# Expert scores by matrix product instead of gathered rows, in a two-block transformer kernel

## The reference

```python
    q = (x @ w_peer_q).reshape(T, PEER_HEADS, PEER_DQ)
    s1, s2 = scores of the two halves of q with keys_1, keys_2      # 128 keys each
    v1, i1 = lax.top_k(s1, 16);  v2, i2 = lax.top_k(s2, 16)
    cand = v1[..., :, None] + v2[..., None, :]
    sc, ci = lax.top_k(cand, 16)
    eidx = e1 * 128 + e2                                            # 128 experts per token
    gates = softmax(sc)
    act = gelu(einsum('td,tkd->tk', xt, peer_u[it]))                # rows of 1024 float32
    y = einsum('tk,tkd->td', gt * act, peer_v[it])
```

## Time and profile before

| | us |
|---|---|
| median of 3 runs | 3166.22 (3160.13 to 3168.16) |
| the profiled execution | 3159.39 |
| its span | 3158.1 |
| TensorE, VectorE, GpSimd, ScalarE busy | 2272.4, 1802.2, 1432.2, 426.0 |
| mean granted TensorE clock | 0.81 |
| moved by DMA | 829.57 MB, of these 539.99 MB by GpSimd's queue |

### The profile page before, as it was taken

One profiled execution on the slowest core, in us unless ns is written; L12 is line 12 of the kernel. 1 busy time (PEld: TensorE's weight loads), 2 busy tenths in 40 slices (PEclk: granted clock), 3 DMA queues, 4 the chain that ended last, 5 costly groups with the idle time before them and its releaser, 6 DMA issues. The chain is left out here.

```text
span 3158.1 us, 24727 instructions
## 1 busy us (share of the span) xinstructions
PE 2272.4 (72%) x8222; PEld 1376.0 (44%) x8222; DVE 1802.2 (57%) x3876; ACT 426.0 (13%) x1209; POOL 1432.2 (45%) x1137
## 2 busy tenths in 40 slices
PE   5997980056673784767674478979957687969989
PEld 3535850023432662322344235758425443437544
DVE  1512119978779677566477897674666854224300
ACT  1212000011200100000000232012000321013310
POOL 0000002377667787778767764676655433100000
PEclk9796995577695796999885557989977688987999
DMA  3310522599889999978889877999998779942376
GB/s 129 121 67 27 173 96 101 157 350 370 282 337 329 333 401 352 321 237 266 293 306 398 288 249 230 394 386 393 363 360 330 259 246 379 340 153 83 126 259 220
DMA packets 291759, 829.57 MB, mean 263 GB/s; under 512 B 23568, under 2 KB 30016, under 8 KB 290864
## 3 DMA queue, kind: packets, MB, share of 16 engines
q0 software_dynamic: 148464, 539.99, 47.7%
q1 hardware_dynamic: 139872, 283.19, 24.7%
q10 hardware_dynamic: 3296, 4.80, 0.4%
HBM read 825.81 MB, written 2.10 MB: 262 GB/s over the span
## 5 line engine op out<-in xcount | busy, mean ns | idle before, releaser
L315 POOL DMA_INDIRECT picks_rows<-peer_u_dram,expert x512 | 723.5, 1413 | 830.2 <-DVE expert L1465 516.2
L315 POOL DMA_INDIRECT picks_rows<-peer_v_dram,expert x512 | 618.1, 1207 | 477.4 <-DVE h L380 354.6
L374 DVE CUSTOM_DVE_ANT_0 picks_rows<-picks_rows,xn 128x1024 f32<-128x1024 f32 x512 | 613.7, 1223 | 169.0 <-DMA picks_rows<-peer_u_dram,expert 144.4
L380 DVE SCALAR_TENSOR_TENSOR h<-picks_rows,picks_weight,h 128x1024 f32<-128x1024 f32 x416 | 535.0, 1286 | 189.4 <-DMA picks_rows<-peer_v_dram,expert 116.3
L465 PE MATMUL psum<-weight_ring,hnT 128*128 128x512 f32 (+4 forms) x576 | 236.9, 573 | 23.0 <-DMA weight_ring<-w_in_dram 10.9
L403 PE MATMUL psum<-picks_rows,picks_diag 128*128 128x512 f32 x384 | 187.3, 625 | 59.9 <-POOL picks_diag L333 59.5
L1753 PE MATMUL psum<-weight_ring,aT 128*128 128x512 f32 x512 | 220.8, 593 | 3.1 <-ACT aT L2060 1.4
L465 PEld LDWEIGHTS psum<-weight_ring,hnT 128*128 128x128 f32 (+1 forms) x576 | 106.2, 187 | 152.4 <-issue 137.5
L874 PE MATMUL psum<-identity_sb,na_probs 128*128 128x128 f32 (+2 forms) x384 | 93.7, 359 | 100.9 <-DVE na_probs L958 79.4
L656 PE MATMUL psum<-identity_sb,n_scaled 128*128 128x128 f32 (+1 forms) x104 | 24.1, 412 | 181.9 <-DVE n_scaled L640 181.9
L1753 PEld LDWEIGHTS psum<-weight_ring,aT 128*128 128x128 f32 x512 | 96.9, 190 | 125.3 <-issue 120.5
(11 more groups left out here) (353 smaller groups left out, 3170.8 us busy)
## 6 DMA issues: line engine op xcount, KB each, us to landing
weight_ring<-w_ff_dram SPq DMA_DIRECT2D x48, 2048.0 KB, 11.0
weight_ring<-w_in_dram SPq DMA_DIRECT2D x44, 2048.0 KB, 13.6
weight_ring<-w_proj_nsa_dram SPq DMA_DIRECT2D x6, 2048.0 KB, 8.1
weight_ring<-w_out_dram SPq DMA_DIRECT2D x6, 2048.0 KB, 14.8
weight_ring<-w_ret_out_dram SPq DMA_DIRECT2D x4, 2048.0 KB, 8.0
weight_ring<-w_mix_out_dram SPq DMA_DIRECT2D x4, 2048.0 KB, 18.9
weight_ring<-w_peer_q_dram SPq DMA_DIRECT2D x4, 2048.0 KB, 13.4
picks_rows<-peer_u_dram,expert POOLq DMA_INDIRECT x512, 7.8
```

The lines of the kernel that those rows point to most:

```text
L315: pool.indirect_dma_start(out=self.rows[:, n % GATHERS, :], out_offset=None, in_=table, in_offset=bass.IndirectOffsetOnAxis(ap=self.expert ...
L374: ins = nc.vector.tensor_tensor_reduce(out=row, in0=row, in1=self.x[t], scale=1.0, scalar=0.0, op0=ALU.mult, op1=ALU.add, accum_out=self.d ...
L380: ins = nc.vector.scalar_tensor_tensor(out=h, in0=row, scalar=self.weight[:, t % 2, k:k + 1], in1=h, op0=ALU.mult, op1=ALU.add)
```

## The change

**Scores.** `peer_select_stage` goes; `experts_stage` does both tiles of a wave. Beside the choice on VectorE, TensorE multiplies the normed tokens with all of `peer_u`, laid out on the host as 32 slabs of 1024 x 512. ScalarE copies each 128 x 512 piece out of PSUM into one of 4 buffers and stores it to a DRAM table, one per tile.

**Gathers.** The `u` gathers of rows and their VectorE steps go. After the stores of a wave have landed, GpSimd gathers the 128 picked scores of each of the two tiles, one float32 per token and DMA, and after these the `v` rows of both tiles. VectorE does all `v` steps; the diagonal products on TensorE and their instructions on GpSimd go. All 8 PSUM banks serve the stages.

**Shares.** The list of steps is 512 long (128 `v` steps per tile). They now belong to m1 to ex of the second wave of the first block (66, 24, 10, 24, 132 steps) and to m2 to nf of the first wave of the second block (36, 24, 10, 83, 96, 7).

```diff
-BANKS = 6
-V_BANKS = (6, 7)
+BANKS = 8
 SHARES = {
-    "sel1": 24, "n1_1": 13, "lat_1": 13, "nq_1": 9, "nkv_1": 9, "up_1": 12, "qk_1": 16, "tq_1": 6, "tk_1": 5, "ma2_1": 26,
...
+    "m1_1": 66, "mix_1": 24, "np_1": 10, "pq_1": 24, "ex_1": 132, "m2_0": 36, "out2_0": 24, "n32_0": 10, "ff12_0": 83,
+    "ff22_0": 96, "nf2_0": 7}
 GATHERS = 8
-DIAGS = 4
-DIAG_LAG = 5
+STAGES = 4
...
+        one += [(("pu", c), a["peer_u"][c], n) for c in range(SLABS)]
...
+    def issue(self, pool, tiles, stored):
+        for signal in stored:
+            pool.wait_ge(*signal)
+        for t in tiles:
+            self.gather_scores(pool, t, range(PICKS))
+        for t in tiles:
+            for k in range(PICKS):
+                self.gather_values(pool, t, k)
...
+    def gather_scores(self, pool, t, picks):
+        for k in picks:
+            if k == 0:
+                pool.wait_ge(self.expert_ready, t + 1)
             pool.indirect_dma_start(
+                out=self.dots[:, t, k:k + 1], out_offset=None, in_=self.scores[t],
+                in_offset=bass.IndirectOffsetOnAxis(ap=self.place[:, t, k:k + 1], axis=0),
+            ).then_inc(self.dots_landed[t], 16)
...
+        def tensor(pe):
+            g.begin(pe)
+            for c, name in enumerate(names):
+                if c == 0:
+                    keys(pe, 0)
+                if c == next_keys and n > 1:
+                    keys(pe, 1)
+                w = g.w.view(name)
+                g.w.arrived(pe, name)
+                for j in range(n):
+                    i = n * c + j
+                    if i >= 4:
+                        pe.wait_ge(*s_copied.after(i - 3))
+                    for k in range(KT):
+                        mm = nc.tensor.matmul(bank(i), xnT[:, k, P * j:P * j + P], w[:, k, :], start=(k == 0), stop=(k == KT - 1))
+                    mm.then_inc(g.w.products_done, 1)
...
+                    nc.scalar.copy(staged[:, i % STAGES, :], bank(i)).then_inc(s_copied.sem, 1)
+                    act.wait_ge(*s_copied.after(i + 1))
+                    rows = g.picks.scores[t].rearrange("(p e) o -> p (e o)", p=P)
+                    act.dma_start(rows[:, 512 * c:512 * c + 512], staged[:, i % STAGES, :]).then_inc(s_stored[i % STAGES].sem, 16)
```

More of the change, by code:

```diff
@@ L267, with __init__ @@
 class Picks:
-    def __init__(self, g, ctx, peer_u, peer_v, expert, gates):
+    def __init__(self, g, ctx, peer_v, scores, expert, place, gates):
         nc, self.g = g.nc, g
@@ L382, in use_to @@
-            ins.then_inc(self.taken["dve"], 1)
-    def add(self, pe, turn=None):
-        self.add_to(pe, self.last if turn is None else self.after(turn - 1))
-    def add_to(self, pe, end):
-        nc = self.g.nc
-        while self.added < end:
-            n = self.added
-            self.added += 1
-            if self.owner[n] != "pe":
-                continue
-            t, _, k = self.steps[n]
-            at = self.number[n] - 1
-            mine = [m for m in range(PICKS) if on_pe(t, m)]
-            if k == mine[0] and self.sums[t]:
-                pe.wait_ge(self.sum_added, self.sums[t])
-            pe.wait_ge(self.landed[n % GATHERS], 16 * (n // GATHERS + 1))
-            pe.wait_ge(self.diag_ready, at + 1)
-            for c, bank in enumerate(V_BANKS):
-                mm = nc.tensor.matmul(self.g.psum[:, bank, :], self.diag[:, at % DIAGS, :],
-                                      self.rows[:, n % GATHERS, 512 * c:512 * c + 512], start=(k == mine[0]), stop=(k == mine[-1]))
-            mm.then_inc(self.taken["pe"], 1)
@@ L407, in finish @@
-    def finish(self, act, dve, pe):
-        t, end = self.finished, 2 * PICKS * (self.finished + 1)
-        assert self.last >= end, (t, self.last)
+            if n:
+                dve.wait_ge(self.taken, n)
+            h = self.g.h[:, t, :]
+            self.g.nc.vector.scalar_tensor_tensor(out=h, in0=self.rows[:, n % GATHERS, :], scalar=self.weight[:, t % 2, k:k + 1],
+                                                  in1=h, op0=ALU.mult, op1=ALU.add).then_inc(self.taken, 1)
+    def finish(self, act, dve):
+        end = PICKS * (self.finished + 1)
+        assert self.last >= end, (self.finished, self.last)
@@ L898, in tensor @@
                 value(pe, s - 2)
-                g.picks.add(pe, 2 * min(s, steps))
-            g.picks.add(pe)
         def exponentials(act, s):
@@ L1477, in peer_select_stage @@
     for signal in (s_scores, s_over, s_exp):
-        signal.count += 1
-    g.ended["pe"], g.ended["act"], g.ended["dve"] = s_scores.after(0), s_exp.after(0), s_link.after(0)
-    g.picks.issue(nc.gpsimd, t)
+        signal.count += n
+    s_copied.count += n * SLABS
+    for i, signal in enumerate(s_stored):
+        signal.count += 16 * len(range(i, n * SLABS, STAGES))
+    g.ended["pe"], g.ended["act"], g.ended["dve"] = g.w.end(names[-1]), s_exp.after(0), s_link.after(0)
+    g.picks.issue(nc.gpsimd, tiles, [signal.after(0) for signal in s_stored])
 def picks_stage(g, tag):
@@ L2062, in second_wave @@
     rows = a["out"].rearrange("(t p) d -> p t d", p=P)
-    norm_stage(g, tag("nf"), [(g.h[:, t, :], P, None) for t in tiles], D, token_out=g.picks.x[first:last],
+    norm_stage(g, tag("nf"), [(g.h[:, t, :], P, None) for t in tiles], D, token_out=[rooms["xn"][:, t, :] for t in tiles],
                gain_rows=tables["g_final"], store=[rows[:, t, :] for t in tiles])
```

296 lines of the change are left out of this document (120 added, 176 removed), and 5 rows, old and new, of the table SHARES.

## The result

The changed kernel takes 3494.7 us (median of 4 runs, 3487.93 to 3495.72), the kernel before 3163.18 beside it: 1.1053 times the time before (95% interval 1.101 to 1.1096). The forecast was 3522, in a range of 3390 to 3660.

What follows compares the result with a forecast made beforehand. No engine was full throughout: TensorE set the pace at both ends, gathered rows and VectorE's picks between. Products (+888 us) and tables (+12), against stretches losing picks and partly waiting for gathers, gave 3522 us, range 3390 to 3660.

Steps and rivals of the forecast that it cites:

- three signs of being wrong: Small gathers above 1.5 us each; a scoring stage not near 444 us; MLP stages of tiles 0 and 1 keeping 224 us.
- step 5: Second block, tiles 0 and 1: merge at 2247 us, MLP stretched to about 335 us, tile 2's wave at 2768.
- Step 1: First scoring stage: products with all of peer_u take 444 us, 470 to 914, hiding DMA and choice; next wave at 935.
- Step 2: Second wave up to its merge, picks taken out: 263 us instead of 438, merge starting at 1198 us.
- Step 3: 256 small gathers ahead of value rows: 1.30 us each, 333 us; rows from 1253, then 85 MB in 230 us.
- Step 4: Second scoring stage: 444 us with 132 picks in it, its transfers of 404 us just hiding; end at 1932.
- Step 6: The last two waves: 369 us for tile 2's wave and 377 us for the last, ending at 3514.
- Rival A: Gathers never show: small ones done before the merges ask, value rows hide; 3249 us, chance 0.09.
- B: Small gathers are slow, up to 2.29 us each, 253 us more a wave: 4028 us, chance 0.10.
- C: Second scoring stage: slabs come late as stores, slabs and rows share engines; 510 instead of 444 us, 3588, chance 0.06.
- E: Scoring products cost one record each, not two; DMA holds the second scoring stage at 404 us; 3262 us, chance 0.02.
- D: TensorE the only bound once picks leave VectorE: 3075 us; faster only if its idle stays within 74 us; chance 0.03.

Runs made afterwards that it cites:

- The plain transfer: Changed kernel with one plain DMA of 128 neighbouring scores per tile instead of the 128 small gathers of picked ones: 3384.76 us, ratio 1.0714.

## Why the prediction was right

3494.7 us lies 27 under the forecast of 3522, and the steps that make up the sum came true, but for one. The prediction named three signs of being wrong, and the third came: the MLP stages kept their pace (step 5).

**Step 1, the products: right.** 444 us forecast a stage, 442 and 444 measured, 2048 records in 880 us, so 16 records in 6.88 us; the clock is 1.00, VectorE's choice and all copies lie beside it. The next wave began at 924, 11 us earlier than I had it: once the last stores had landed (917), exponential, gates and norm took 6.6 us where I had 15.

**Step 2, the stages without picks: right in kind, 18 us long.** Merge after 245 us from the first transposes (263 forecast). The longer keys in attention cost 9 us (54.9 against 46) where I added 17; the rest of the 18 I did not trace.

**Step 3, the small gathers: right.** 0.963 us on average and 0.30 behind, 1.26 against 1.30; the value rows at 1249.06 against 1253; VectorE's standstill from 1187 to 1253. Then I had 85 MB at 369 GB/s in 230 us. It was 208 us at 371 GB/s, so 77 MB; I take it that part of the slabs was there already. The plain transfer shows what this step costs the end, 110 us.

**Step 4: right.** 444 us with 132 picks in it, at 348 GB/s.

**Step 5: the sum right, the place wrong.** The merge came at 2176, not 2247: 20 us from the start of the stage, 12 because the gap behind the scoring stage was 23 us and not 35, and 40 because the stages without picks took 240 us where I took 280, near the lower bound of 237. This was one bad term, and it cost nothing: the first row is asked for at 2252 either way, 333 us of small gathers behind the scoring stage as forecast, and VectorE waited 64 us for it instead of the 8 that I had. The gathers of GpSimd were on the path. From there to tile 2's wave it took 486 us at 346 to 397 GB/s, forecast 497. But here the place was wrong. I had the MLP stretched to 335 us, and it took 226 at full pace, as in the kernel before (224): ScalarE drains its products, VectorE only does picks there, and slabs arrive in time. The deficit of picks showed as 116 us of idle TensorE behind the MLP. So the picture of a TensorE slowed by the picks inside the MLP is wrong, and the sum survived it for a reason and not by luck: the forecast of 497 us rests on the bytes, and these have to move before tile 2's wave wherever TensorE waits. Shares that move picks past that border get at the gap: 116 us became 13.

**Step 6: 367 and 382 us against 369 and 377.**

Rival A (gathers hide) failed on the queue, B (2.29 us each) on 0.963, C on the 444 us with rows and slabs together, E on 2048 records. D needs an idle TensorE of no more than 74 us; the kernel without picks, the best case of D, is at 3170 and no faster than before. Of the 27 us by which the span was forecast too long, 20 are there by the second scoring stage (4 at the rows, 16 behind them), 10 more by tile 2's wave, and the last two waves give 3 back.

One reading of mine does not carry over. I put the 1.99 us of a gather beside picks down to VectorE, with the Trainium skill (GPSIMD Engine Reference, section Specifications) behind it. GpSimd of the changed kernel, 44 us apart, beside VectorE's picks:

```profile
2628.64 1.73 POOL L311 DMA_INDIRECT picks_rows<-peer_v_dram,expert  x1 [0.30 <-issue]
...
2672.82 1.09 POOL L311 DMA_INDIRECT picks_rows<-peer_v_dram,expert  x1 [0.30 <-issue]
```

VectorE was busy 15.4 of 24 us beside the slow ones (2624 to 2648) and 22.2 of 24 beside the fast ones (2656 to 2680), so it is not what made them slow. What changed between them is that the last slab had landed. Until then slabs and rows shared the engines evenly (850 packets each from 2636 to 2648), and behind it only rows moved (1345 packets from 2656 to 2668). So most of a slow gather here goes with slabs in the transfers beside the rows, and the rule on the shared interfaces does not explain it. It may still hold for the 1.99 us of the earlier trace rows: there no slab moved (845 packets from 618 to 630, all of GpSimd's queue, at 257 GB/s), and no run tests that row.

## What to carry to other kernels

Before gathered rows are replaced by a dense product, compare it with what those rows cost the end (a run without them: 368 us) and not with their busy time or bytes: 682 us of a full engine can't win there, whatever is hidden. A gather's price on GpSimd is a turn in its queue, 1.25 us for 4 bytes a partition as for 4 KB while the transfers are not full, and small ones ahead of the rows delay everything behind them. Placing work in an in-order row pays only once its data can be there: the same shares cost 64 us with late rows (3494.7 to 3558.8), and with the order of the gathers changed they gained 68 (3446.2 to 3378.4).

## What the runs showed of the hardware that I had not expected

TensorE can start one record per 2.80 us, whatever its size, for 70 us and more at a time. It did so in the profiled execution of the kernel with half the products (the other one was 18 us shorter, so it must have too), at a granted clock of 0.50 in the worst stretch, the lower of the two levels. It came behind either scoring stage, beside small gathers issued every 1.25 us. It did not come in the same kernel with a pause between gathers (1.84 us, one run), nor without gathers, nor in the changed kernel, whose gathers are as dense. A stage of half the products moves 369 GB/s at a DMA share of 0.98, the changed kernel's stages 186 at 0.51 and 348 at 0.88; whether that matters, no run tells, but by itself it does not bring it on, since the same stage with plain scores had no standstill behind it.

A second one: indirect gathers of 512 bytes and of 512 KB leave GpSimd equally fast, 0.94 and 0.95 us, as long as the transfers are not full.
